# Tokens outermost in the second-key one-hot table of a mixture-of-keys layer

## What is computed

```
    sc, sel = lax.top_k(cand, PEER_TOPK)
    eidx = jnp.take_along_axis(cidx, sel, axis=-1)
    gates = jax.nn.softmax(sc, axis=-1)
...
        uc = u_emb[ic]
        act = jax.nn.gelu(jnp.einsum('cd,ced->ce', xc, uc))
        vc = v_emb[ic]
        return jnp.einsum('ce,ced->cd', (gc * act).astype(vc.dtype), vc)
```

## Time and profile before

| | |
|---|---|
| median of 3 runs | 3813.81 us (3813.74 to 3813.82) |
| profiled execution, device time | 3801.99 us |
| profiled execution, span of the trace | 3800.3 us |
| PE busy | 3480.4 us, 92% of the span |
| DVE busy | 2231.6 us, 59% |
| ACT busy | 1650.7 us, 43% |
| POOL busy | 712.1 us, 19% |
| mean granted TensorE clock | 0.957 of full speed |

### The profile page before, as it was taken

One profiled execution on the slowest core, in us unless ns is written; L12 is line 12 of the kernel. 1 busy time (PEld: TensorE's weight loads), 2 busy tenths in 40 slices (PEclk: granted clock), 3 DMA queues, 4 the chain that ended last, 5 costly groups with the idle time before them and its releaser, 6 DMA issues.

```text
span 3800.3 us, 70644 instructions
## 1 busy us (share of the span) xinstructions
PE 3480.4 (92%) x24282; PEld 3152.3 (83%) x24282; DVE 2231.6 (59%) x3351; ACT 1650.7 (43%) x2238; POOL 712.1 (19%) x648
## 2 busy tenths in 40 slices
PE   7964899999999999999999979999997997998986
PEld 6953799999989998899888858997775777977975
DVE  4544539266677667766666764335654776544454
ACT  4444446533453334433333545664433444334443
POOL 1300008810111001100000106882112111100010
PEclk9977999999999999999999989999998998999998
DMA  6501455555686568755545854564442675764522
GB/s 198 175 24 33 161 171 155 166 181 181 209 264 215 180 186 256 252 177 181 155 149 162 264 180 133 178 184 147 141 143 92 231 265 185 244 187 144 182 94 89
DMA packets 181810, 656.45 MB, mean 173 GB/s; under 512 B 23040, under 2 KB 23184, under 8 KB 180576
## 3 DMA queue, kind: packets, MB, share of 16 engines
q1 hardware_dynamic: 149328, 545.82, 45.5%
q0 software_dynamic: 32400, 109.56, 9.3%
HBM read 653.18 MB, written 2.10 MB: 172 GB/s over the span
## 4 chain that ended last, share of the span: by engine, by line
PE 83%; DVE 6%; ACT 3%; issue 3%; POOL 2%; PEld 2%; DMA 1%; DVEq 0%; ACTq 0%; SPq 0%; POOLq 0%; PEldq 0%
PE PS L526 13%; PE PS L527 13%; PE PS L528 13%; PE PS L780 6%; PE PS L782 6%; PE PS L784 6%; PE PS L733 5%; PE PS L578 3%; PE PS L582 3%; PE PS L580 3%; PE PS L561 2%; PE PS L562 2%; PE PS L563 2%; POOL w_lo L427 2%; PE PS L934 1%
## 5 line engine op out<-in xcount | busy, mean ns | idle before, releaser
L1044 ACT ACTIVATE w_hi<-raw 128x1024 fp32r<-128x1024 f32 x1032 | 1093.3, 1060 | 1796.2 <-PE PS L528 1041.4
L1438 DVE TENSOR_TENSOR w_lo<-raw,w_hi 128x1024 fp32r<-128x1024 f32 x872 | 1076.6, 1235 | 1037.2 <-ACT w_hi L1044 1026.6
L526 PE MATMUL PS<-xt_hi,w_hi 128*128 128x256 f32 x4608 | 1324.7, 287 | 34.2 <-DVEq L1883 8.5
L527 PE MATMUL PS<-xt_lo,w_hi 128*128 128x256 f32 x4608 | 1308.6, 284 | 0.0
L528 PE MATMUL PS<-xt_hi,w_lo 128*128 128x256 f32 x4608 | 1308.3, 284 | 0.0
L526 PEld LDWEIGHTS PS<-xt_hi,w_hi 128*128 128x128 f32 x4608 | 891.0, 193 | 46.6 <-issue 35.9
L527 PEld LDWEIGHTS PS<-xt_lo,w_hi 128*128 128x128 f32 x4608 | 889.6, 193 | 0.0
L528 PEld LDWEIGHTS PS<-xt_hi,w_lo 128*128 128x128 f32 x4608 | 888.9, 193 | 0.0
L427 POOL TENSOR_TENSOR w_lo<-raw,w_hi 128x1024 fp32r<-128x1024 f32 x160 | 403.1, 2545 | 240.4 <-ACT w_hi L1044 240.3
L780 PE MATMUL PS<-w_hi,st_hi 128*128 128x512 f32 x1024 | 404.2, 395 | 0.2
L782 PE MATMUL PS<-w_hi,st_lo 128*128 128x512 f32 x1024 | 400.6, 391 | 0.0
(11 more groups left out here) (362 smaller groups left out, 3505.9 us busy)
## 6 DMA issues: line engine op xcount, KB each, us to landing
raw<-in_u_emb SPq DMA_DIRECT2D x256, 512.0 KB, 3.5
raw<-in_v_emb SPq DMA_DIRECT2D x256, 512.0 KB, 4.2
ada<-in_ada_w POOLq DMA_DIRECT2D x240, 256.0 KB, 3.7
raw<-in_xbc SPq DMA_DIRECT2D x96, 512.0 KB, 3.6
raw<-in_z SPq DMA_DIRECT2D x80, 512.0 KB, 3.5
raw<-in_q SPq DMA_DIRECT2D x64, 512.0 KB, 3.5
raw<-in_a_out SPq DMA_DIRECT2D x64, 512.0 KB, 4.9
raw<-in_k SPq DMA_DIRECT2D x48, 512.0 KB, 4.2
```

The source lines that it names most:

```text
L526: pe.matmul(o, w_h, x_h, start=start, stop=False, skip_group_check=True)
L527: pe.matmul(o, w_h, x_l, start=False, stop=False, skip_group_check=True)
L1044: act.activation(w_hi[:, u, :], raw[:, u, :], ACT.Copy).then_inc(hi_done, 1)
L1438: dve.tensor_tensor(w_lo[:, u, :], raw[:, u, :], w_hi[:, u, :].bitcast(F32), ALU.subtract)\
```

## The change

The two second-key tables change their order in memory: 8 tokens outermost, 32 keys innermost. The number of elements, the values, and the order of instructions on every engine stay as they are. ACT writes the key numbers once (128 per partition) where it wrote each eight times (1024). `hot1` is not touched.

In the comparison of L1706 the slot's key no longer varies along the innermost dimension but repeats over 32 elements (a step of 0), and in the product of L1715 so does the gate. The other input and the output are contiguous. The moving operand of L733 becomes 32 contiguous elements.

```diff
-        iota8 = sb("iota8", [P, NK, 8], BF16, experts)
+        iota_b = sb("iota_b", [P, NK], BF16, experts)
         hot1 = sb("hot1", [P, 2, 4, NK, 2], BF16, experts)
         iota2 = sb("iota2", [P, NK, 2], BF16, experts)
-        hot2 = sb("hot2", [P, 2, EB, 8], BF16, experts)
-        hot2_gate = sb("hot2_gate", [P, 2, 3, EB, 8], BF16, experts)
+        hot2 = sb("hot2", [P, 2, 8, EB], BF16, experts)
+        hot2_gate = sb("hot2_gate", [P, 2, 3, 8, EB], BF16, experts)
...
                         last = pe.matmul(PS[:, bank, t * EB:(t + 1) * EB], hot1[:, r, t // 2, :, t % 2],
-                                         hot2_gate[:, r, part, :, t], start=part == 0, stop=part == 2,
+                                         hot2_gate[:, r, part, t, :], start=part == 0, stop=part == 2,
                                          skip_group_check=True)
...
-            act.activation(iota8[:, :, :], cc[:, CC["iota"]:CC["iota"] + NK].unsqueeze(2).to_broadcast([P, NK, 8]),
-                           ACT.Copy)
+            act.activation(iota_b[:, :], cc[:, CC["iota"]:CC["iota"] + NK], ACT.Copy)
...
-                dve.tensor_tensor(hot2[:, r, :, :], iota8[:, base:base + EB, :],
-                                  slotsT[:, 1, ds(8 * n, 8)].unsqueeze(1).to_broadcast([P, EB, 8]),
+                dve.tensor_tensor(hot2[:, r, :, :], iota_b[:, base:base + EB].unsqueeze(1).to_broadcast([P, 8, EB]),
+                                  slotsT[:, 1, ds(8 * n, 8)].unsqueeze(2).to_broadcast([P, 8, EB]),
                                   ALU.is_equal).then_inc(sem("keys_matched"), 1)
...
-                shape = [P, 3, EB, 8]
+                shape = [P, 3, 8, EB]
                 dve.tensor_tensor(hot2_gate[:, r, :, :, :], hot2[:, r, :, :].unsqueeze(1).to_broadcast(shape),
-                                  slot_gate[:, :, ds(8 * n, 8)].unsqueeze(2).to_broadcast(shape), ALU.mult)\
+                                  slot_gate[:, :, ds(8 * n, 8)].unsqueeze(3).to_broadcast(shape), ALU.mult)\
                     .then_inc(sem("hot_done"), 1)
```

## The result

The changed kernel takes 3712.96 us (median of 4 runs, 3710.17 to 3716.37) against 3813.77 us before (4 runs, 3813.26 to 3813.82): a ratio of 0.9737, interval 0.9725 to 0.9749, or 101 us less.

A forecast was written before the change was run, and what follows sets the result against it. PE was taken to bound the kernel where tables are built. -79 us (PE) + 2 (edges) = -77, from 3801.99 to 3725, plus 12 to the median: 3737 us; range 3706 to 3817, own case 3710 to 3765.

The forecast's parts named there:

- PE sets the pace where tables are built: Stages up1 and down2: PE busy 238.40 of 240.00 and 224.63 of 230.00 us, other engines wait for it.
- The moving stream, by its step of 8, holds L733 back; not the weight load, not the issue: L733: step of 8 elements (16 bytes) sets 59 ns a matmul; the rival that the stream isn't it had chance 0.20.
- The reading of single starts: L733 trace: loads start with the matmul ahead, their matmul 0.06 us later, against 0.03 us where one column streams.
- The pace after: 0.033 us: L733 matmuls after the change: 0.033 us each, expected between 0.030 and 0.040, wider bounds 0.02 and 0.050 us.
- the PE term: L733: a group takes 0.79 us in place of 1.41, 0.62 us less, and 128 groups give 79 us.
- the line through 128 and 256 columns: Matmul pairs 0.07 and 0.12 us apart: about 0.4 ns a column, so 32 contiguous columns should take 0.03 us.
- the first pair of the old group: First two L733 matmuls of a group, 0.040 us apart, the shortest distance of this kind, taken as the pace's upper end.
- DVE: 0.545 us a group, the f32 rate: L1706 133 ns and L1715 412 ns dearer at the f32 rate, together 70 us of DVE in 128 groups.
- Hidden in the loops by 2.41 us of idle time, of which about 1.2 are left: DVE's idle end of each half body: PE saves 0.62 of 2.41 us, and 0.545 fit with 1.2 us to spare.
- 2 us at the edges: PE waiting for DVE's tables at the first group and the last ones: 2 us added in all.
- Key numbers on ACT: nothing: Smaller fill of key numbers, less than the 1.06 us of now, once, where ACT has slack: no effect.
- 12 us between the profiled execution and the median: Profiled execution 3801.99 us, median 3813.81: the difference was added to the sum of 3725, giving 3737 us.

The follow-up runs named there:

- the two halves of the change: Kernel before, L733 reading contiguous elements of the old table: 3705.0 us; changed kernel, L733 reading every eighth element of the new table: 3817.29 us.
- the experiment with two more products: Changed kernel with two more gate products a group on DVE, written where nobody reads: 3789.57 us in a single run.
- pairs: Changed kernel with second-key tables in pairs of tokens (step 2), gate product split in three: 3708.9 us, again 3709.51 us beside 3713.82 us.
- two kernels: The changed kernel, 3713.82 us, and the one with second-key tables in pairs of tokens, 3709.51 us, run side by side.

## Why the prediction was right, and where it was off

- *PE sets the pace where tables are built.* Right. 101 us taken from L733 came out as 96 us of the stretch, and half a body shortened by 0.78 us, nearly the 0.79 of the group.
- *The moving stream, by its step of 8, holds L733 back; not the weight load, not the issue.* Right, and shown by the two halves of the change, by 103 and 101 us. (It holds for a load at step 2. At step 8 the load sets a pace of 62 ns by itself.) The reading of single starts, a load that begins with the matmul ahead of it and a matmul that waits 0.06 us in place of 0.03, picked the right operand.
- *The pace after: 0.033 us.* The term that was off. It is 0.0256 us, 0.614 us a group where I had 0.79, so a group saves 0.79 us in place of the 0.62 forecast, and the PE term is 128 x 0.79 = 101 us where I had 79. The value lies inside the bounds (0.020 to 0.050). What failed is the choice between the ends: the line through 128 and 256 columns (0.030) and the first pair of the old group (0.040) both speak of streams, and the new pace is no stream but a floor, the same for 16 columns. The first pair was doubly unfit: its matmuls still had the step of 8.
- *DVE: 0.545 us a group, the f32 rate.* Right: 134 and 400 ns, where 133 and 412 were put.
- *Hidden in the loops by 2.41 us of idle time, of which about 1.2 are left.* 1.29 us are left, and the experiment with two more products shows that it is this gap that hides it. That the number fits is partly luck: with the 0.79 us that PE really saved, the same working leaves 1.08 us. The other 0.2 us come from a pause of DVE ahead of the group's second `w_lo`, which I hadn't counted as cover: from the start of `apply` (L1723 before, L1722 after) to the start of that `w_lo` it was 0.53 us before and is 0.33 us after, in the half bodies shown:

```profile
1214.94 0.41 DVE L1723 TENSOR_TENSOR hid<-hid,PS 128x256 f32 x1
1215.47 1.23 DVE L1438 TENSOR_TENSOR w_lo<-raw,w_hi 128x1024 fp32r<-128x1024 f32 x1
```

```profile
1201.58 0.41 DVE L1722 TENSOR_TENSOR hid<-hid,PS 128x256 f32 x1
1201.91 1.22 DVE L1437 TENSOR_TENSOR w_lo<-raw,w_hi 128x1024 fp32r<-128x1024 f32 x1
```

- *2 us at the edges.* Too low. PE's idle time before L733 grew by 5.8 us: 2.5 us by the dearer tables (10.4 with them alone), and 2.7 us because PE itself is faster and arrives earlier at the same tables (10.6 with the old tables); 0.6 us more come only with both. I had priced only the first of the two, and not the granted clock: with the dearer tables come another 3 us (slow PE) to 4.5 us (fast PE) of PE's busy time.
- *Key numbers on ACT: nothing.* Nothing in the rows speaks against it; it wasn't tried alone.
- *12 us between the profiled execution and the median.* I added all of it. The changed kernel's profiled execution was at its median, so against the traces alone the change is 89 us, and 101 by the medians. The 89 us are the 96 of the stretch less the 7 by which its first L733 comes later. Of the 12 us between 89 and 101, these 7 are so accounted for; the other 5 are open, since no trace of the kernel before at its median was kept. So of the 24 us between the forecast and the result, the pace explains 22, the edges take 4 back, and some 6 us are in neither.

## What to carry to other kernels

Look at the step of both operands of a short matmul: with 2-byte elements a step of 8 doubles the price of a 32-column matmul with its load, from 26 to 59 ns, a step of 4 makes it 33 ns, and a step of 2 costs nothing above the floor. A table that two engines share need not be contiguous for either: pairs give PE its full pace and leave DVE the fast form of its 16-bit instructions, which it lost here when an input repeated along the innermost dimension (284 to 418 ns for 256 elements, 684 to 1220 ns for 1024). Before making DVE's work dearer, read the gap in its timeline after the gain, not before, and expect the edges of stages to give some back, also because the faster engine arrives earlier.

Where an effect is a few microseconds, read PE's busy time over the same stretch as well as its waits. Here 3.6 of the 5.5 us between two kernels were the same matmuls at a lower granted clock, and no wait showed them.

## What was unexpected of the hardware

- A pair of weight load and matmul has a floor of 25.6 ns for 16 and for 32 contiguous columns; 64 columns take 29.6 ns (0.71 us by 24).
- The stationary operand at step 8 costs 62 ns for 128 columns, about as much as the moving operand does for 32 (59 ns).
- Of the moving operand, step 4 costs 33 ns: the price shows above the floor from somewhere between 4 and 8 bytes on.
- The granted clock fell to 0.50 for pieces of mostly 3 to 4 us in the stretch, five times in the changed kernel and three times with pairs, the same count when each was run again.
- The table instructions had single executions of 2.5 to 2.9 us in the rows of before, of the changed kernel and of both halves of it, among them one of 2871 ns for an instruction that takes 684. What lengthens them is open; it wasn't tried.
